# An input projection in halves of 256 columns in place of whole slabs of 512

## The chip, the core and the metric

The program runs on one NeuronCore of a Trainium2 chip, in one launch. What counts is its device time in microseconds: the median of the runs before is 2477.26 us (2477.15 and 2477.36). TensorE multiplies a stationary block (the weights, loaded by an instruction of their own) by moving columns and adds into PSUM banks of 512 float32 columns. VectorE (DVE), ScalarE (ACT) and GpSimd (POOL) do the rest of the arithmetic, and SyncE (SP) orders most of the transfers.

## The reference, cut to what matters

One layer of a decoder. The 2048 prompt tokens and 8 sample tokens are normalised, modulated and projected; the projection's columns are q, k, v, an output gate, two gate rows, u and vs. A chunked mLSTM and a gated chunk-MLP mix them, then come an output projection and a SwiGLU:

```python
h = rmsnorm(x, g_norm1) * (1 + sc1) + sh1
proj = h @ w_in
q, k, vm, o, ig, fg, u, vs = split_cols(proj, IN_SIZES)
...
x = x + gt1 * (mix @ w_out)
h2 = rmsnorm(x, g_norm2) * (1 + sc2) + sh2
a, bb = jnp.split(h2 @ w_gate_up, 2, axis=-1)
x = x + gt2 * ((jax.nn.silu(a) * bb) @ w_down)
```

Everything is float32. D_MODEL is 1024, and `w_in` without its gate columns has 3072 columns.

## The kernel before, in words

The prompt is worked through in four blocks of 512 tokens (`BLK`). Block 0 and block 3 are written out, blocks 1 and 2 are a loop over the same code. The normalised input of a block lies transposed in SBUF, as `hT`, eight tiles (`KT`) of 128 features by 512 tokens. Each float32 factor is kept as a sum of two parts of type float32r, `hi` and `lo`, and a product is made of three matmuls: lo x hi, hi x lo and hi x hi.

A **slab** is 128 columns of a weight matrix with all 1024 rows, 512 KB. SP loads it into one of two slots of `raw` (line 438); ACT rounds it into `w_hi` (line 848); DVE subtracts and gives `w_lo` (line 1337). TensorE waits for that (`slab_ready`), and for the bank to be free (`evac`), and multiplies the slab with the block's 512 tokens into one of two PSUM banks, `G[0]` or `G[1]`. For each of the eight feature tiles these are the three matmuls of `product` (lines 1862 to 1864), 24 in all with 512 moving columns each; every matmul has its own load of 128 x 128 weights. The last one signals `slab_used`, on which ACT's evacuation of the bank and the next use of the slot wait.

The input projection has 24 such slabs per block, and in block 0 the first of them is part of `first_products`, which goes its own way. The order of a block is written out in two lists, `PRE` and `MIX`: the numbers 0 to 23 are slabs (`mix_slab`), and between them stand the steps of the token mixing, among them `chunk_a` (transposes of k at line 2004, scores at 2030), `chunk_b` (lines 2039 to 2046), `spatial` (line 2061) and `finish_heads` (line 2071):

```python
PRE = [0, 1, 2, 3, "R1", 4, "V0", "R2", 5, "V1", "R3", 6, "V2", 7, "R4", "V3", 8, 9, "COL", 10, "WD", 11]
MIX = ["A0", 12, "B0", 13, "A1", 14, "B1", 15, "A2", "GV", 16, "B2", 17, "VST", 18, "A3", 19, "SO", "B3",
       20, "CMS", "CU0", 21, "CU1", "ML", 22, "CU2", 23, "CU3"]
```

So slabs fill TensorE while the other engines do the steps between. The two up projections use the same `product`, 44 slabs per block; output and down projections have a form of their own (lines 1915 to 1917) with the tokens as the stationary part. Small float32 matmuls outside these products appear in the trace as pairs of instructions, transposes as single ones. In block 3 the sample tokens' work is spread between the slabs.

Of the kernel before, what the change touches and what calls it, by code (L numbers as in the profile page):

```python
# [31 lines left out]
KT = D // P  # L32
SEQ = 2048
BLK = 512
# [73 lines left out]
def hybrid_step(nc, x_prompt, x_sample, c_prompt, c_sample, state_C, state_n, state_m, w_ada, b_ada,  # L108
# [4 lines left out]
    with ctx:  # L113
# [7 lines left out]
        def new(name, shape, dt):  # L121
            n = 4 if dt != BF16 else 2
            for s in shape[1:]:
                n *= s
            at = top[0]
            align = 128 if n >= P else 32
            at = top[0] = (at + align - 1) // align * align
            top[0] += (n + 31) // 32 * 32
            return place(name, shape, dt, at), at


        hT_hi, HT = new("hT_hi", [P, KT, BLK], F32R)
        hT_lo, HL = new("hT_lo", [P, KT, BLK], F32R)
# [8 lines left out]
        w_hi, WH = new("w_hi", [P, 2, KT, P], F32R)  # L142
        w_lo, WL = new("w_lo", [P, 2, KT, P], F32R)
# [48 lines left out]
        half, _ = new("half", [P, 32], F32)  # L192
# [89 lines left out]
        G = bank[0:2]  # L282
# [26 lines left out]
        def signal(name, per, before=0):  # L309
            return Signal(sem(name), per, before)  # L310
# [5 lines left out]
        slab_used = signal("slab_used", NSLAB, 1)  # L316
# [1408 lines left out]
        def _(pe):  # L1725
            mm = pe.matmul
# [3 lines left out]
            for k in range(KT):  # L1730
                ins = pe.transpose(T[0][:, k * R:(k + 1) * R], xs[:, k * P:(k + 1) * P], ident[0:R, 0:R])
# [124 lines left out]
            def product(out, slot, rhs_hi, rhs_lo, tiles, start=True, stop=True, before_tile=None):  # L1856

                for n, (k, r) in enumerate(tiles):
                    if before_tile is not None:
                        before_tile(k)  # L1860
                    last = n == len(tiles) - 1
                    mm(out, w_lo[:, slot, k, :], rhs_hi[:, r, :], start=start and n == 0, stop=False)  # L1862
                    mm(out, w_hi[:, slot, k, :], rhs_lo[:, r, :], start=False, stop=False)  # L1863
                    ins = mm(out, w_hi[:, slot, k, :], rhs_hi[:, r, :], start=False, stop=stop and last)  # L1864
                return ins

            every = [(k, k) for k in range(KT)]

            def raw_ready(blk, s, j=0):
                pe.wait_ge(raw_in[s % 2].sem, raw_in[s % 2].at(blk, 16 * (s // 2 + 1)) + j)  # L1870

# [57 lines left out]
            def slab_ready(blk, s, j=0):  # L1929
                pe.wait_ge(lo_done.sem, lo_done.at(blk, s + 1) + j)  # L1930
# [143 lines left out]
            def mix_slab(blk, s):  # L2074
                slab_ready(blk, s)
                if s == 0:
                    pe.wait_ge(out_read.sem, out_read.at(blk, 0))
                pe.wait_ge(evac.sem, evac.at(blk, max(s - 1, 0)))
                product(G[s % 2][:, :], s % 2, hT_hi, hT_lo, every).then_inc(slab_used.sem, 1)

            pe.sem_inc(out_read.sem, 1)
            pe.sem_inc(evac.sem, 1)
# [5 lines left out]
            def pe_block(blk, last, first=False):  # L2088
# [4 lines left out]
                for step in PRE + MIX:  # L2093
                    if isinstance(step, int):
                        if not (first and step == 0):
                            mix_slab(blk, step)
                        if first:
                            modulation(step)
                        for piece in SAMPLES.get(step, ()) if last else ():
                            for_samples(piece)  # L2100
                    elif step in ("COL", "WD", "VST", "CMS", "ML"):
                        handlers[step](blk)
                    elif step[0] == "V":
                        v_tokens(blk, int(step[1]))
                    elif step[0] == "A":
                        chunk_a(blk, int(step[1]))
                    elif step[0] == "B":
                        chunk_b(blk, int(step[1]))

                pe.wait_ge(evac.sem, evac.at(blk, N_WIN - 1))  # L2110
                for n in range(N_OUT):
                    j, q = divmod(n, OUT_Q)
                    if last:
                        if n == 0:
                            pe.wait_ge(cms_read.sem, cms_read.at(blk, H))
                            pe.wait_ge(sem("s_ready"), 1)
                        if n % 2 == 0:
                            for r in (q, q + 1):
                                raw_ready(blk, S_OUT + n + r - q)
                                sample_pairs(N2, r % 2, s_mixp, 2 * r, j, r == 0, r == OUT_Q - 1)  # L2120
                    slab_ready(blk, S_OUT + n)
                    for i in range(TT):
                        ready = None
                        if n == 0 and i == TT - 1:
                            pe.wait_ge(evac.sem, evac.at(blk, N_WIN))
                        if n < OUT_Q and i == 0:
                            def ready(k):
                                done = mix_ready if k < H else cu_ready
                                pe.wait_ge(done.sem, done.at(blk, k % H + 1))
                        if n == 0 and i == 1:  # L2130
                            pe.wait_ge(mix_ready.sem, mix_ready.at(blk, 2))
                        if n == OUT_Q:
                            pe.wait_ge(out_read.sem, out_read.at(blk, i + 1))
                        ins = tile_product(OUT_BANK[i][:, :], n % 2, mix_hi, mix_lo, 2 * q, i, q == 0,
                                           q == OUT_Q - 1, before_k=ready)
                        if q == OUT_Q - 1 and i < TT - 1:
                            ins.then_inc(tile_ps.sem, 1)
                    ins.then_inc(slab_used.sem, 1)
# [4 lines left out]
                def up_four(half_i, begin):  # L2143
                    for pair in range(2):
                        slabs, n = half_i * 4, half_i * 2
                        for u in range(2):
                            c = 2 * pair + u
                            sample_at = -1 if not last or u == 1 else 1 if begin and c == 0 else 0

                            def samples():  # L2150
                                for r in (c, c + 1):
                                    raw_ready(blk, S_UP + r, half_i * 32)
                                    sample_columns(SP_[:, r * P:(r + 1) * P], r % 2, s_hp)

                            if sample_at == 0:
                                samples()
                            slab_ready(blk, S_UP + c, slabs)
                            if u == 0:
                                pe.wait_ge(evac.sem, evac.at(blk, N_WIN + pair) + n)
                                pe.wait_ge(silu_done.sem, silu_done.at(blk, pair) + n)  # L2160
                                def ready(k):
                                    if last and begin and pair == 0 and k == KT - 2:
                                        sample_sum(EP_[:, KT * NB:])
                                    pe.wait_ge(h_ready.sem, h_ready.at(blk, k + 1))
                                product(G[0][:, :], 0, hT_hi, hT_lo, every, before_tile=ready)\
                                    .then_inc(slab_used.sem, 1)
                            else:
                                pe.wait_ge(gated.sem, gated.at(blk, pair) + n)
                                product(G[1][:, :], 1, hT_hi, hT_lo, every).then_inc(slab_used.sem, 1)
                            if sample_at == 1:  # L2170
                                pe.wait_ge(sem("s_ready"), 2)
                                samples()
# [17 lines left out]
                for n in range(N_DOWN):  # L2190
                    j, q = divmod(n, DOWN_Q)
                    def samples():
                        for r in (n, n + 1):
                            raw_ready(blk, S_DOWN + r)
                            jr, qr = divmod(r, DOWN_Q)
                            sample_pairs(SP_, r % 2, s_actp, 2 * qr, jr, qr == 0, qr == DOWN_Q - 1)
# [33 lines left out]
            for k in range(KT):  # L2230
                ins = pe.transpose(NT_BANK[k // 4][0:NB, (k % 4) * P:(k % 4 + 1) * P], s_h32[:, k, :],
                                   ident[:, :])
# [30 lines left out]
```

## Time and profile before

| | us |
|---|---|
| runs, median of 2 | 2477.26 |
| runs, lowest and highest | 2477.15, 2477.36 |
| profiled execution, span | 2477.8 |
| TensorE busy with matmuls | 2427.0 |
| TensorE busy with weight loads | 1979.9 |
| DVE busy | 1203.8 |
| ACT busy | 846.1 |
| POOL busy | 176.9 |

The profiled execution has no other time of its own than its span, from its first to its last instruction. The page gives busy times, the chain of work that ended last, and groups of instructions by line; the trace behind it answers by stretches (windows), by waits, and instruction by instruction (timeline). PE is TensorE's matmuls and PEld its weight loads, which overlap with matmuls. A matmul lasts from its start to the end of its results; neighbours overlap, so the distance of two starts, and not the duration, tells how many of them fit in a microsecond.

### The profile page before, as it was taken

The page shows a single profiled execution, that of the slowest core. Times are in us where ns is not written, and L with a number is a line of the kernel's source. Part 1 is how long each engine was busy: PE and PEld are TensorE (multiplying, and loading weights), DVE is VectorE, ACT ScalarE, POOL GpSimd, SP SyncE. Part 2 cuts the span into 40 slices and gives each one's busy share as a digit, 9 for nine tenths or more (in the row PEclk, how much of TensorE's full clock was granted, in tenths as well). Part 3 has the DMA queues.
Part 4 walks back from the last instruction along what each step waited for, and adds up shares of the span by engine and source line. Part 5 has one row for each costly group of instructions (what it writes and reads, how often), then busy time and mean ns, then how long its engine had stood idle before and what let it go on. Part 6 is the DMA issues. An engine that isn't in the chain of part 4 may idle for free.

```text
span 2477.8 us, 32788 instructions
## 1 busy us (share of the span) xinstructions
PE 2427.0 (98%) x12296; PEld 1979.9 (80%) x12296; DVE 1203.8 (49%) x1773; ACT 846.1 (34%) x1152; POOL 176.9 (7%) x143
## 2 busy tenths in 40 slices
PE   5999999999999999999999999999999999999998
PEld 4688877888888878888888878888888878888776
DVE  4648544434346554444354754443449754333323
ACT  2333422233244243334143343333236323333212
POOL 0022000000003000000002200000002400000001
PEclk8999999999999999999999999999999999999999
DMA  7822365332352333332342233333255322222222
GB/s 280 287 80 90 111 196 164 118 95 96 91 147 66 101 111 99 96 93 94 103 140 78 90 111 98 97 93 102 94 185 160 92 77 69 85 85 85 89 90 86
DMA packets 361045, 280.14 MB, mean 113 GB/s; under 512 B 11289, under 2 KB 302653, under 8 KB 360920
## 3 DMA queue, kind: packets, MB, share of 16 engines
q1 hardware_dynamic: 333012, 228.91, 30.5%
q10 hardware_dynamic: 23956, 34.81, 4.1%
q0 software_dynamic: 3968, 14.95, 1.6%
q8 instruction: 71, 1.16, 0.2%
q14 instruction: 38, 0.30, 0.0%
HBM read 267.68 MB, written 10.96 MB: 112 GB/s over the span
## 4 chain that ended last, share of the span: by engine, by line
PE 89%; DVE 5%; issue 2%; DMA 2%; ACT 1%; POOL 0%; DVEq 0%; SPq 0%; ACTq 0%; POOLq 0%
PE banks L1862 18%; PE banks L1863 18%; PE banks L1864 18%; PE banks L1915 9%; PE banks L1916 8%; PE banks L1917 8%; PE banks L1742 1%; DVE w_lo L1337 1%; DMA stage<-in_w_ada_dram 1%; PE banks L1876 1%; PE banks L2004 1%; PE banks L2061 1%; PE banks L1886 1%; PE banks L1938 1%; PE banks L2030 1%
## 5 line engine op out<-in xcount | busy, mean ns | idle before, releaser
L1862 PE MATMUL banks<-hT_hi,w_lo 128*128 128x512 f32 x2176 | 859.9, 395 | 3.1 <-DVE hT_lo L1343 1.6
L1864 PE MATMUL banks<-hT_hi,w_hi 128*128 128x512 f32 x2176 | 848.6, 390 | 0.0
L1863 PE MATMUL banks<-hT_lo,w_hi 128*128 128x512 f32 x2176 | 848.5, 390 | 0.0
L1337 DVE TENSOR_TENSOR w_lo<-raw,w_hi 128x1024 fp32r<-128x1024 f32 x392 | 493.3, 1258 | 579.5 <-ACT w_hi L848 567.7
L848 ACT ACTIVATE w_hi<-raw 128x1024 fp32r<-128x1024 f32 x392 | 412.7, 1053 | 465.7 <-PE banks L1917 437.4
L1862 PEld LDWEIGHTS banks<-hT_hi,w_lo 128*128 128x128 f32 x2176 | 409.3, 188 | 100.6 <-issue 9.3
L1864 PEld LDWEIGHTS banks<-hT_hi,w_hi 128*128 128x128 f32 x2176 | 409.0, 188 | 86.2
L1863 PEld LDWEIGHTS banks<-hT_lo,w_hi 128*128 128x128 f32 x2176 | 409.4, 188 | 81.3
L1915 PE MATMUL banks<-w_lo,act_hi 128*128 128x512 f32 x704 | 276.2, 392 | 0.0
L1916 PE MATMUL banks<-w_hi,act_lo 128*128 128x512 f32 x704 | 274.2, 390 | 0.0
L1917 PE MATMUL banks<-w_hi,act_hi 128*128 128x512 f32 x704 | 274.1, 389 | 0.0
L1675 DVE TENSOR_TENSOR work<-work,banks 128x512 f32<-128x512 f32 x88 | 60.5, 688 | 271.9 <-ACT work L971 271.9
L977 ACT ACTIVATE act_hi<-work 128x512 f32 (+1 forms) x88 | 55.6, 632 | 371.8 <-DVE work L1679 371.8
L1915 PEld LDWEIGHTS banks<-w_lo,act_hi 128*128 128x128 f32 x704 | 132.1, 188 | 32.0 <-issue 4.5
L1917 PEld LDWEIGHTS banks<-w_hi,act_hi 128*128 128x128 f32 x704 | 132.1, 188 | 27.8
L1916 PEld LDWEIGHTS banks<-w_hi,act_lo 128*128 128x128 f32 x704 | 132.2, 188 | 26.7
L1679 DVE TENSOR_TENSOR work<-work,banks 128x512 f32<-128x512 f32 x88 | 60.6, 689 | 190.1 <-PE banks L1864 190.1
L587 POOL TENSOR_TENSOR rrt<-msq,half 128x1 f32<-128x1 f32 (+1 forms) x27 | 18.2, 676 | 1424.2 <-DVE msq L1098 1168.2
L971 ACT ACTIVATE work<-banks 128x512 f32<-128x512 f32 x88 | 52.6, 598 | 187.3 <-PE banks L1864 186.9
L1915 PE MATMUL banks<-w_lo,mix_hi 128*128 128x512 f32 x256 | 100.4, 392 | 1.8 <-DVE w_lo L1337 1.1
L1916 PE MATMUL banks<-w_hi,mix_lo 128*128 128x512 f32 x256 | 99.8, 390 | 0.0
L1917 PE MATMUL banks<-w_hi,mix_hi 128*128 128x512 f32 x256 | 99.6, 389 | 0.0
(335 smaller groups left out, 1828.9 us busy)
## 6 DMA issues: line engine op xcount, KB each, us to landing
raw<-in_w_gate_up_dram SPq DMA_DIRECT2D x176, 512.0 KB, 3.6
raw<-in_w_in_dram SPq DMA_DIRECT2D x96, 512.0 KB, 3.7
raw<-in_w_down_dram SPq DMA_DIRECT2D x88, 512.0 KB, 3.6
ada_stage<-in_w_ada_dram ACTq DMA_DIRECT2D x8, 2048.0 KB
raw<-in_w_out_dram SPq DMA_DIRECT2D x32, 512.0 KB, 3.6
in_stage<-in_w_in_dram ACTq DMA_DIRECT2D x6, 2048.0 KB
stage<-in_w_ada_dram SPq DMA_DIRECT2D x4, 2048.0 KB
x_sb<-in_x_prompt_dram POOLq DMA_DIRECT2D x4, 2048.0 KB, 8.8
```

The lines of the kernel that those rows point to most:

```text
L848: act.activation(w_hi[:, s % 2], raw[:, s % 2], ACT.Copy).then_inc(hi_done.sem, 1)
L971: act.activation(work[:, 2], G[0][:, :], ACT.Sigmoid).then_inc(evac.sem, 1)
L977: act.activation(act_hi[:, bass.ds(pair_i * 2 + u, 1), :], work[:, 3:4, :], ACT.Copy)\
L1337: ve.tensor_tensor(w_lo[:, s % 2], raw[:, s % 2], w_hi[:, s % 2].bitcast(F32), ALU.subtract).then_inc(lo_done.sem, 1)
L1675: ve.tensor_tensor(work[:, 2], work[:, 2], G[0][:, :], ALU.mult).then_inc(silu_done.sem, 1)
L1679: ve.tensor_tensor(work[:, 3], work[:, 2], G[1][:, :], ALU.mult).then_inc(gated.sem, 1)
L1862: mm(out, w_lo[:, slot, k, :], rhs_hi[:, r, :], start=start and n == 0, stop=False)
L1863: mm(out, w_hi[:, slot, k, :], rhs_lo[:, r, :], start=False, stop=False)
L1864: ins = mm(out, w_hi[:, slot, k, :], rhs_hi[:, r, :], start=False, stop=stop and last)
L1915: mm(out, x_hi[:, k0 + k, t], lo[:, k, :], start=start and k == 0, stop=False)
L1916: mm(out, x_lo[:, k0 + k, t], hi[:, k, :], start=False, stop=False)
L1917: ins = mm(out, x_hi[:, k0 + k, t], hi[:, k, :], start=False, stop=stop and k == 1)
```

## The change

A new function, `half_product`, does what `product` does for a slice `t` of the block's tokens. `mix_slab` calls it twice: with tokens 0 to 255 over all eight feature tiles, then with tokens 256 to 511. Both write into their own half of the same bank, and the signal `slab_used` comes from the last matmul of the second half. A slab is then 48 matmuls of 256 moving columns, each with its own load. Each block of weights is loaded twice per slab. The first slab of block 0, the gate rows, and the output, up and down projections stay as they are.

```diff
+            def half_product(out, slot, t):
+
+                for k in range(KT):
+                    mm(out[:, t], w_lo[:, slot, k, :], hT_hi[:, k, t], start=k == 0, stop=False)
+                    mm(out[:, t], w_hi[:, slot, k, :], hT_lo[:, k, t], start=False, stop=False)
+                    ins = mm(out[:, t], w_hi[:, slot, k, :], hT_hi[:, k, t], start=False, stop=k == KT - 1)
+                return ins
+
...
                 pe.wait_ge(evac.sem, evac.at(blk, max(s - 1, 0)))
-                product(G[s % 2][:, :], s % 2, hT_hi, hT_lo, every).then_inc(slab_used.sem, 1)
+                for half in range(2):
+                    ins = half_product(G[s % 2], s % 2, slice(half * BLK // 2, (half + 1) * BLK // 2))
+                ins.then_inc(slab_used.sem, 1)
```

On TensorE, between step B0 and the next step, slab 13 of block 0 stands so before (the first row belongs to B0; w_lo and w_hi are the weights, hT the moving tokens):

```order
L2046 MATMUL banks<-vg,k_tm 128x129 x3
L1862 MATMUL banks<-hT_hi,w_lo 128x512 [waits evac,lo_done]
L1863 MATMUL banks<-hT_lo,w_hi 128x512
L1864 MATMUL banks<-hT_hi,w_hi 128x512
L1862 MATMUL banks<-hT_hi,w_lo 128x512
```

and so in the changed kernel, in which the lines behind the new function are eight higher:

```order
L2054 MATMUL banks<-vg,k_tm 128x129 x3
L1872 MATMUL banks<-hT_hi,w_lo 128x256 [waits evac,lo_done]
L1873 MATMUL banks<-hT_lo,w_hi 128x256
L1874 MATMUL banks<-hT_hi,w_hi 128x256
L1872 MATMUL banks<-hT_hi,w_lo 128x256
```

The three rows come 8 times before and 16 times now, with the waits on the first row alone; nothing stands between the halves. The order on DVE, ACT and SP is the same in both kernels.

Where the first slab of block 0 ends and the second begins, the changed kernel has, on TensorE (the rows with 512 columns are the end of `first_products`):

```order
L1863 MATMUL banks<-hT_lo,w_hi 128x512
L1864 MATMUL banks<-hT_hi,w_hi 128x512
L1759 MATMUL banks<-ident,w_raw 128x128 [waits h32,ws_masked]
L1759 MATMUL banks<-ident,w_raw 128x128 x3
L1872 MATMUL banks<-hT_hi,w_lo 128x256 [waits evac,lo_done]
```

There only the last row is new in form: it was L1862 with 128x512.

## Rows read from the trace of the kernel before

**Rows 1.** The page's first part: busy us (share), instructions of each engine.

```profile
PE 2427.0 (98%) x12296; PEld 1979.9 (80%) x12296; DVE 1203.8 (49%) x1773; ACT 846.1 (34%) x1152; POOL 176.9 (7%) x143
```

**Rows 2.** The page's chain that ended last: shares by engine, by line.

```profile
PE 89%; DVE 5%; issue 2%; DMA 2%; ACT 1%; POOL 0%; DVEq 0%; SPq 0%; ACTq 0%; POOLq 0%
PE banks L1862 18%; PE banks L1863 18%; PE banks L1864 18%; PE banks L1915 9%; PE banks L1916 8%; PE banks L1917 8%; PE banks L1742 1%; DVE w_lo L1337 1%; DMA stage<-in_w_ada_dram 1%; PE banks L1876 1%; PE banks L2004 1%; PE banks L2061 1%; PE banks L1886 1%; PE banks L1938 1%; PE banks L2030 1%
```

**Rows 3.** Windows over the input projections of block 0 and block 3.

```profile
core 0: us, PE busy (x) PEld busy (x) DVE busy (x) ACT busy (x) POOL busy (x), PEclk, DMA share, GB/s
58.86:235.73 176.87, 175.48 (x971) 136.26 (x969) 118.09 (x204) 63.38 (x92) 32.92 (x23) 0.99 0.48 151
...
1827.96:1993.25 165.29, 161.88 (x824) 135.44 (x822) 132.64 (x259) 82.90 (x142) 48.52 (x31) 0.99 0.49 150
```

**Rows 4.** TensorE's waits: waiter, whom it waited for, us, times, longest.

```profile
PE banks L2061 <- DVEq L1422: 2.6, 4, 0.7
PE banks L2046 <- POOL vg L674: 2.0, 1, 2.0
...
PE banks L1862 <- DVE w_lo L1337: 0.8, 4, 0.3
```

**Rows 5.** Timeline of TensorE in undisturbed slabs: start us, duration us, instruction.

```profile
899.65 0.39 PE L1864 MATMUL banks<-hT_hi,w_hi 128*128 128x512 f32 x1
899.88 0.39 PE L1862 MATMUL banks<-hT_hi,w_lo 128*128 128x512 f32 x1
...
944.08 0.39 PE L1862 MATMUL banks<-hT_hi,w_lo 128*128 128x512 f32 x1
```

**Rows 6.** Timeline of TensorE in slab 3 of block 0.

```profile
87.05 0.63 PE L1863 MATMUL banks<-hT_lo,w_hi 128*128 128x512 f32 x1
87.48 0.63 PE L1864 MATMUL banks<-hT_hi,w_hi 128*128 128x512 f32 x1
```

**Rows 7.** Windows around rows 5 and 6; the number behind POOL's is PEclk.

```profile
899.65:944.08 44.43, 44.43 (x198) 36.79 (x196) 18.74 (x22) 15.70 (x19) 0.00 (x0) 1.00 0.34 99
...
86.20:89.10 2.90, 2.90 (x8) 2.31 (x7) 2.55 (x5) 0.00 (x0) 0.00 (x0) 0.50 1.05 396
```

**Rows 8.** Timeline at a slab's end: its last matmul, and the next load.

```profile
92.44 0.39 PE L1864 MATMUL banks<-hT_hi,w_hi 128*128 128x512 f32 x1
...
92.76 0.12 PEld L1742 LDWEIGHTS banks<-ada_stage,hTs 128*9 128x9 f32 x8 [0.35 <-issue]
```

**Rows 9.** Timeline of small float32 matmuls with 129 and with 8 columns.

```profile
745.39 1.06 PE L2042 MATMUL banks<-CN,qT 128*128 128x129 f32 x8
746.28 1.06 PE L2046 MATMUL banks<-vg,k_tm 128*128 128x129 f32 x8
...
2079.80 0.95 PE L1904 MATMUL banks<-ssel,s_ev 128*128 128x8 f32 x8
2080.68 1.08 PE L1876 MATMUL banks<-raw,s_hp 128*32 128x128 f32 x32
```

**Rows 10.** Groups of weight loads by form: busy us, mean ns of one.

```profile
L1862 PEld LDWEIGHTS banks<-hT_hi,w_lo 128*128 128x128 f32 x2176 | 409.3, 188 | 100.6 <-issue 9.3 <-DVE hT_lo L1343 6.1 <-DVE w_lo L1337 3.2
...
L1904 PEld LDWEIGHTS banks<-ssel,s_ev 128*128 128x128 f32 x88 | 11.5, 191 | 0.8
```

**Rows 11.** Timeline: a matmul, and the load for the matmul behind it.

```profile
911.21 0.39 PE L1864 MATMUL banks<-hT_hi,w_hi 128*128 128x512 f32 x1
...
911.21 0.19 PEld L1862 LDWEIGHTS banks<-hT_hi,w_lo 128*128 128x128 f32 x1
```

**Rows 12.** Timeline of TensorE after a wait: the first and last of eleven matmuls.

```profile
1929.16 0.39 PE L1864 MATMUL banks<-hT_hi,w_hi 128*128 128x512 f32 x1
...
1931.47 0.39 PE L1862 MATMUL banks<-hT_hi,w_lo 128*128 128x512 f32 x1
```

**Rows 13.** The page's groups that split a slab on DVE and ACT.

```profile
L1337 DVE TENSOR_TENSOR w_lo<-raw,w_hi 128x1024 fp32r<-128x1024 f32 x392 | 493.3, 1258 | 579.5 <-ACT w_hi L848 567.7
L848 ACT ACTIVATE w_hi<-raw 128x1024 fp32r<-128x1024 f32 x392 | 412.7, 1053 | 465.7 <-PE banks L1917 437.4
```

## The prediction, made before the changed kernel ran

> **What bounds the kernel now.** I read the page's busy times first, then the chain of waits, then the windows of the input projections, then TensorE's waits, and last single matmuls in the timeline. TensorE is busy 98% of the span [rows 1], and the chain that ended last runs for 89% over it [rows 2]. In the stages that the change touches it is the same: TensorE works 175.48 of 176.87 us in token block 0 and 161.88 of 165.29 in block 3, while DVE, the next engine, reaches at most 132.64 [rows 3]. What it waits for there is small: 2.6 us in four places for a DVE chain (line 1422), 2.0 us once for POOL's vg, 0.8 us for four slabs whose lo part came late, 0.3 the longest [rows 4]. So a nanosecond more or less in a slab's matmuls is a nanosecond of the kernel, almost without cover.
>
> A busy PE is not yet TensorE at its peak, so the price of one matmul must be read from starts, not from the 0.39 us that it lasts. In a long stretch of undisturbed slabs the first of 197 matmuls starts at 899.65 us and the last at 944.08 [rows 5]: 44.43 / 196 = 226.7 ns per 512 columns. The granted clock is 1.00 there [rows 7], the level of 2.4 GHz, at which 512 columns need 213.3 ns. So each matmul takes **13.4 ns beyond its columns**, and the whole question is what becomes of these 13.4 ns when a matmul has 256 columns.
>
> **The change part by part.** It adds no work of arithmetic, no DMA and no wait: each slab of the steps 0 to 23 does 48 matmuls of 256 columns in place of 24 of 512, each with its own load of 128 x 128 weights. First_products keeps step 0 of block 0 as it was. That leaves 23 + 3 x 24 = 95 slabs, 95 x 24 = 2280 matmuls that become 4560.
>
> *The matmuls.* If the 13.4 ns come once per matmul, a half takes 256 / 2.4 + 13.4 = 106.7 + 13.4 = 120.0 ns, a pair 240.0, and the change costs 2280 x (240.0 - 226.7) = **+30.4 us**. If they come with the columns, a half takes 113.3 ns and the change costs nothing. Three rows bear on it. In a stretch in which the granted clock is 0.50 [rows 7], the level of 1.2 GHz, the same matmuls start 0.43 us apart [rows 6]: that is 512 / 1.2 = 427 ns with nothing on top. So the 13.4 ns are no cycles of the array, neither per matmul nor per column; something that feeds the array needs about 227 ns and shows only at the full clock. And it is not the load of the next weights that gets in the way: the last matmul before some small ones, with no load behind it for 0.35 us, still lasts 0.39 us [rows 8]. After an interruption the distance is larger before it settles: ten steps from 1929.16 to 1931.47 us, 231 ns each [rows 12]. A rate per column would hardly change so, a start-up of each matmul could; I take the fixed cost, and keep the rate as a rival.
>
> *The loads.* A load begins when the matmul before it begins [rows 11] and today has 226.7 ns; it will have 120. Nearest rows: eight matmuls of 8 columns each take 2080.68 - 2079.80 = 0.88 us, eight of 129 columns 0.89 us [rows 9], 110 to 111 ns each, each with its own 128 x 128 load. With so different columns the same distance means that the load sets it. These are plain float32, but their loads last as long, 191 ns against 188 [rows 10]. So loads follow each other every 111 ns, which fits under 120 with 9 ns to spare: nothing added. The bounds of a half are then 111 ns (below, if the 13.4 ns vanish beside the load) and 129 ns (above, 111 and then 231 - 213.3 = 17.7, if the start-up follows the load and never settles).
>
> *Issue.* TensorE gets 2280 more pairs of load and matmul. The rows with 129 columns issue a pair in 111 ns [rows 9]; at 120 this is covered, and at worst it is the same 111.
>
> *The neighbours.* The semaphores fire where they did, after the last matmul of a slab, so ACT evacuates the whole bank as before. A slab grows from 24 x 226.7 = 5.44 to 5.76 us. Splitting the next one takes 1.05 us on ACT and 1.26 on DVE [rows 13], and its raw data was ordered one slab earlier: more covered than before, cost nothing; without that cover a late slab would cost at most those 2.3 us. What a longer slab gives back is waits: in front of line 2061 one slab lies between the DVE chain's start and its use, so 4 x 0.32 = 1.3 us, the longest late lo part 0.3, and POOL's vg up to 2.0 [rows 4]. Between nothing and -3.6 us I take **-2.5**, since POOL's chain is in part tied to DVE's order in the same slabs.
>
> *Sum.* +30.4 - 2.5 = +28 us on the profiled execution's span of 2477.8, 2505.7 us. Its span lies 0.5 us over the median of the runs, 2477.26, so **2505 us**, 1.1% more. A change of 2% is 49.5 us; about that is what a measurement of this kernel can tell from no change.
>
> **The rule against it.** The row says 226.7 ns for 512 columns, 13.4 more than they need. The Trainium skill, TensorE: Matmul & The Clock Gate, section Back-to-back issue gap, gives a warm matmul N / 2.4 + 2.5 ns, 216 for 512 columns; the trace disagrees by 11 ns. By that rule a half would take 109.2 ns, an estimate, and the load would be the longer of the two. What that would do here is the second rival.
>
> **The rivals.**
> 1. *The extra is a rate.* 113.3 ns per half, 0 us for the matmuls, -1 for waits: 2476. For it speaks that a matmul with no load behind it is stretched as much as the others [rows 8]; against it the unequal 231 and 227 ns [rows 5, 12].
> 2. *The loads set the pace, a little faster.* If a half carries almost no start-up, it waits for its load: 111.5 ns, 223 a pair, 2280 x -3.7 = -8 us, 2469. For it speak the narrow matmuls, in which nothing beyond the load shows [rows 9]; against it that the start-up of float32r at full clock is seen in every settled row [rows 5].
> 3. *The start-up comes behind the load: slower.* Today the next load is long done when a matmul ends; with 111 ns of load beside 107 of columns it is the last to arrive, and if a matmul's start-up can only begin then, a half takes 111 + 13.4 = 124 ns, or 129 with the 17.7 ns of the unsettled steps [rows 12]. Place: each half of the 95 slabs. Price: with the middle, 126.5, a pair takes 253, 2280 x 26.3 = +60, less 2.5 for waits, 2535 (2525 to 2545 with the two ends). It decides from 125 ns per half: then 4560 x 4.8 = 22 us come on top of 2505 and 2% are reached. For it speaks that nothing in the rows shows a float32r matmul that waits for its load; against it that rows of 129 columns, as close to their loads, keep an even 111 [rows 9].
> 4. *Load and matmul follow each other.* 111 + 120 = 231 per half, 2280 x 235 = +537 us, 3014. Against it stand rows 9, with half that distance.
>
> That the change does not do what it says is out: the order shows 256 columns in all of these slabs.
>
> **How the numbers follow.** The fixed cost, 2505: 0.58. Rival 1, 2476: 0.20. Rival 2, 2469: 0.06. Rival 3, 2535: 0.12. Rival 4: 0.04. The likeliest gives the predicted time; its own range is 2503 to 2508 (waits between -3.6 and nothing, on 2477.3 + 30.4). The range over the cases goes from 2469 (rival 2) to 2535 (the middle of rival 3) and leaves out half of rival 3, rival 4 and what lies under rival 2. Within 2%: the fixed cost, rivals 1 and 2, and the lower end of rival 3, which crosses the border at 2527: 0.87. Slower by over 2%: the rest of rival 3 and rival 4: 0.12. Faster by over 2%: no row shows a way to -50 us; 0.01.
>
> **What would show it.** In the changed kernel's timeline the starts within an input slab should be 120 ns apart, a slab 5.76 us long, and the 512-column stages unchanged at 226.7 ns. Loads should start with the matmul before them, 188 ns long, and not end the wait of a matmul. The windows of the four projections should be longer by 7 to 8 us each, and the waits on lines 2061 and 2046 (of before) shorter. Starts 113 ns apart make rival 1 right, 111 with matmuls lengthened by their loads rival 2, 124 to 129 rival 3. The prediction is wrong in its central step if the half's extra is not 13 ns.

## The result, and the profile after

The changed kernel takes 2499.86 us (2499.14 and 2500.58) against 2477.26: ratio 1.0086, interval 1.0056 to 1.0115. That is 22.6 us more, where 28 were predicted; the profiled executions, 2477.8 and 2499.1 us, differ by 21.3. The forecast of 2505 us is 5 us high: the time lies within the range over the cases, 2469 to 2535, and 3 us under the likeliest case's own, 2503 to 2508. The mechanism behind it did not hold in the same way: the 13 ns per half are there, but they are no fixed cost of a matmul, and the weight loads have a part in them.

First the page of the changed kernel: busy times, the chain that ended last by engine and by line, and one of the new lines' groups.

```profile
PE 2452.6 (98%) x14576; PEld 2101.1 (84%) x14576; DVE 1211.8 (48%) x1773; ACT 846.3 (34%) x1152; POOL 170.5 (7%) x143
...
PE 91%; DVE 4%; issue 2%; DMA 2%; ACT 1%; POOL 0%; DVEq 0%; SPq 0%; ACTq 0%; POOLq 0%
...
L1872 PE MATMUL banks<-hT_hi,w_lo 128*128 128x256 f32 x1520 | 436.2, 287 | 1.1 <-DVE w_lo L1337 1.0
...
L1872 PEld LDWEIGHTS banks<-hT_hi,w_lo 128*128 128x128 f32 x1520 | 291.3, 192 | 2.7 <-DVE w_lo L1337 1.6
```

There are 2280 more matmuls and as many more loads than in [rows 1], and the chain runs over TensorE for 91% where it was 89% [rows 2]. A load lasts 192 ns, 188 before [rows 10].

The price is read from starts. In the timeline of TensorE (start us, duration us, instruction) the first two rows are the ends of 24 undisturbed steps in a slab of block 1, the last two those of 190 steps in an up projection:

```profile
677.02 0.28 PE L1872 MATMUL banks<-hT_hi,w_lo 128*128 128x256 f32 x1
...
679.90 0.28 PE L1872 MATMUL banks<-hT_hi,w_lo 128*128 128x256 f32 x1
...
899.80 0.39 PE L1862 MATMUL banks<-hT_hi,w_lo 128*128 128x512 f32 x1
...
942.88 0.39 PE L1863 MATMUL banks<-hT_lo,w_hi 128*128 128x512 f32 x1
```

2.88 / 24 = 120.0 ns per half, and 43.08 / 190 = 226.7 ns per 512 columns, as in [rows 5]. Of all 4560 halves, 4106 are followed by the next matmul after 120 ns. So a pair costs 240.0 - 226.7 = 13.3 ns, and 2280 pairs 30.4 us, as the prediction had it.

Timeline of the weight loads in the same slab:

```profile
676.91 0.19 PEld L1872 LDWEIGHTS banks<-hT_hi,w_lo 128*128 128x128 f32 x1
677.03 0.19 PEld L1873 LDWEIGHTS banks<-hT_lo,w_hi 128*128 128x128 f32 x1
```

The matmul of line 1872 starts at 677.02 and the load for the next one, of line 1873, at 677.03: load and matmul start together, as in [rows 11]. The next matmul starts at 677.14, before the 0.19 us of its load are over on record, so that duration can't tell whether a matmul waits for its load. In a kernel with matmuls of 128 columns (below) they start some 60 ns after their loads; here it is 117, so the halves are not held back by their own loads in that way.

TensorE's waits after (waiter, whom it waited for, us, times, longest), where they changed:

```profile
PE banks L1742 <- DMA stage<-in_w_ada_dram: 12.4, 3, 7.6
...
PE banks L2069 <- DVEq L1422: 1.2, 3, 0.4
PE banks L1872 <- DVE w_lo L1337: 1.0, 1, 1.0
PE banks L2054 <- POOL vg L674: 0.9, 1, 0.9
```

Lines 2069 and 2054 are 2061 and 2046 of before. The DVE chain's 2.6 us fell to 1.2 and POOL's 2.0 to 0.9 [rows 4]. The wait for the adaptive weights, at the very start, was 9.8 us in two places before and is 12.4 in three; a third one of 3.1 us was put down to DVE before.

Last the windows (us; then busy time and count of PE, PEld, DVE, ACT, POOL; granted clock; DMA share; GB/s): the projection of block 0, the slab of block 0 in which [rows 6] lie, and the projection of block 3.

```profile
60.31:241.05 180.74, 179.82 (x1520) 165.23 (x1519) 120.01 (x204) 63.38 (x92) 29.88 (x23) 1.00 0.47 148
87.60:90.50 2.90, 2.90 (x25) 2.90 (x26) 2.58 (x4) 0.00 (x0) 0.00 (x0) 1.00 0.96 350
1845.60:2014.95 169.35, 166.87 (x1399) 165.22 (x1397) 135.44 (x260) 83.06 (x142) 50.52 (x31) 1.00 0.48 146
```

The two projections take 180.74 and 169.35 us against 176.87 and 165.29 [rows 3], 3.9 and 4.1 more. The middle row stands for something that was not in the sum: before, the granted clock was 0.50 here (1.2 GHz) [rows 7], after it is 1.00 (2.4 GHz). In the trace of before TensorE had just done small matmuls and a wait of 0.57 us; block 3 had a second such stretch, after the wait of 2.0 us for POOL:

```profile
1925.70:1929.10 3.40, 3.40 (x13) 3.03 (x13) 1.75 (x3) 0.00 (x0) 3.32 (x4) 0.50 0.55 148
```

In these two stretches 512 columns started 427 ns apart instead of 227, and in the second the small matmuls of line 2046 were slower too, some 1.6 us lost in each. The changed kernel's profiled execution has neither.

**Where the time went.** From the first gate matmul to the first one of the output projection the four blocks grew by 3.84, 6.16, 6.07 and 4.06 us, 20.1 together; the start before them grew by 1.45, the end lost 0.45, and the stages between grew by 0.13. In the start it is not the waits for the adaptive weights, 12.9 us before with the one on DVE and 12.4 after: the three groups of 16 matmuls on these weights took 10.7 us against 9.1. The change doesn't touch them, and why they took longer is not shown. Of the four blocks' 20.1 us, +30.4 are the pairs; -3.7 are TensorE's waits there, 8.4 us before and 4.7 after; -3.2 are the two stretches at the lower clock. The rest, -3.4, is seen in the steps after each interruption, which have not yet settled to one distance. In the input projections of before, 388 such steps of 512 columns took 231.5 ns on average, 1.9 us in all over 226.7; after, 325 such halves took 118.2, 0.6 us in all under 120.0. That makes -2.5; the other -0.9 lies in the first and last steps of the slabs, beside other matmuls. Two of the rows:

```profile
1845.60 0.28 PE L1872 MATMUL banks<-hT_hi,w_lo 128*128 128x256 f32 x1
...
1846.90 0.28 PE L1874 MATMUL banks<-hT_hi,w_hi 128*128 128x256 f32 x1
```

These are 11 steps, some 118 ns each, behind the gate matmuls of block 3; the unsettled steps of [rows 12] took 231. A settled pair costs 13.3 ns, an unsettled one 2 x 118.2 - 231.5 = 4.9. Block 1 has no stretch at the lower clock and is closed by itself: 576 x 13.33 = 7.68 for the pairs, -0.54 for unsettled steps, -0.82 for waits, -0.16 for first and last steps and the small matmuls, together 6.16, by which the block grew.

### The profile page after: what moved, and what is told of

Read it like the earlier page. It is cut to its first block, busy times and chain, and to the rows that moved or that the text cites. A ratio compares the mean times of both kernels' runs of the same rounds, so it can differ in the third digit from the quotient of the medians.

```text
span 2499.1 us, 37348 instructions
## 1 busy us (share of the span) xinstructions
PE 2452.6 (98%) x14576; PEld 2101.1 (84%) x14576; DVE 1211.8 (48%) x1773; ACT 846.3 (34%) x1152; POOL 170.5 (7%) x143
## 4 chain that ended last, share of the span: by engine, by line
PE 91%; DVE 4%; issue 2%; DMA 2%; ACT 1%; POOL 0%; DVEq 0%; SPq 0%; ACTq 0%; POOLq 0%
PE banks L1862 13%; PE banks L1863 13%; PE banks L1864 13%; PE banks L1923 9%; PE banks L1925 8%; PE banks L1924 8%; PE banks L1872 6%; PE banks L1874 6%; PE banks L1873 6%; PE banks L1742 1%; DMA stage<-in_w_ada_dram 1%; PE banks L1884 1%; DMA raw<-in_w_in_dram 1%; DVE w_lo L1337 1%; PE banks L2012 1%
## 5 line engine op out<-in xcount | busy, mean ns | idle before, releaser
L1862 PE MATMUL banks<-hT_hi,w_lo 128*128 128x512 f32 x1416 | 556.0, 393 | 2.9 <-DVE hT_lo L1343 1.6
L1863 PE MATMUL banks<-hT_lo,w_hi 128*128 128x512 f32 x1416 | 551.2, 389 | 0.0
L1864 PE MATMUL banks<-hT_hi,w_hi 128*128 128x512 f32 x1416 | 551.2, 389 | 0.0
L1872 PE MATMUL banks<-hT_hi,w_lo 128*128 128x256 f32 x1520 | 436.2, 287 | 1.1 <-DVE w_lo L1337 1.0
L1874 PE MATMUL banks<-hT_hi,w_hi 128*128 128x256 f32 x1520 | 429.9, 283 | 0.0
L1873 PE MATMUL banks<-hT_lo,w_hi 128*128 128x256 f32 x1520 | 429.9, 283 | 0.0
L1862 PEld LDWEIGHTS banks<-hT_hi,w_lo 128*128 128x128 f32 x1416 | 265.8, 188 | 71.1 <-issue 8.5
L1864 PEld LDWEIGHTS banks<-hT_hi,w_hi 128*128 128x128 f32 x1416 | 265.8, 188 | 55.6
L1863 PEld LDWEIGHTS banks<-hT_lo,w_hi 128*128 128x128 f32 x1416 | 265.9, 188 | 53.4
L1872 PEld LDWEIGHTS banks<-hT_hi,w_lo 128*128 128x128 f32 x1520 | 291.3, 192 | 2.7 <-DVE w_lo L1337 1.6
L1873 PEld LDWEIGHTS banks<-hT_lo,w_hi 128*128 128x128 f32 x1520 | 291.5, 192 | 0.1
L1874 PEld LDWEIGHTS banks<-hT_hi,w_hi 128*128 128x128 f32 x1520 | 291.3, 192 | 0.0
L1675 DVE TENSOR_TENSOR work<-work,banks 128x512 f32<-128x512 f32 x88 | 60.6, 688 | 271.9 <-ACT work L971 271.9
```

The costliest lines, as they stand in the source:

```text
L1675: ve.tensor_tensor(work[:, 2], work[:, 2], G[0][:, :], ALU.mult).then_inc(silu_done.sem, 1)
L1872: mm(out[:, t], w_lo[:, slot, k, :], hT_hi[:, k, t], start=k == 0, stop=False)
L1873: mm(out[:, t], w_hi[:, slot, k, :], hT_lo[:, k, t], start=False, stop=False)
L1874: ins = mm(out[:, t], w_hi[:, slot, k, :], hT_hi[:, k, t], start=False, stop=k == KT - 1)
```

## The experiments

They were to tell whether the 13.3 ns of a pair are a start-up of each matmul, a pace of the loads, or something else, and whether the order of the halves or the place in the block matters. In all of them the slabs of the input projection alone are changed, unless the text says otherwise, and in the block order of before. A settled distance is one that repeats, within 1 ns, through a run of equal matmuls; steps that hold an interruption are left out of the means.

**The change once more**, beside kernels that do a part of it. No edit: it is the changed kernel.

> The changed kernel again, beside the kernel before, for a narrower interval: 21 to 24 us slower. If the shares that I read from the two traces are right (2280 matmuls doubled at +13.3 ns a pair, +30.4 us; less about 3 to 4 us of waits, about 3 us of stretches at the half clock, about 3 us of settling after interruptions), its trace shows the same shares again, and the stretch at a granted clock of 0.50 in slab 3 of block 0 is missing again.

2498.99 us against 2479.69, ratio 1.0082 (1.0065 to 1.0099), +19.3. The blocks grew by 3.81, 6.14, 6.05 and 1.32 us: the same as above but in block 3, where TensorE's waits are 0.5 us against 2.4 in the first execution of the changed kernel and 3.4 in that of before. So the change costs 19 to 23 us, less than the 21 to 24 expected here, and block 3 carries most of the scatter. The stretch at 0.50 in block 0 is missing again. (It lies in slab 4, the first behind the step R1; [rows 6] and the expectations call it slab 3.)

**Half of the slabs in halves**, the first twelve of a block or the last twelve:

```diff
-                product(G[s % 2][:, :], s % 2, hT_hi, hT_lo, every).then_inc(slab_used.sem, 1)
+                for lo, hi in ((0, 256), (256, 512)) if s < 12 else ((0, 512),):
+                    ins = half_product(G[s % 2], s % 2, slice(lo, hi))
+                ins.then_inc(slab_used.sem, 1)
```

> Halves only in slabs 0 to 11, the ones ahead of the token mixing; slabs 12 to 23 whole, as before. Start-up theory: 47 slabs x 24 x 13.3 ns = +15.0 us. The slabs of this part are interrupted about as often as the others, so they get back 1 to 2 us of settling, and the stretch at the half clock in slab 3 of block 0 (1.5 us) if that is due to the halves. Little of the waits, which lie behind slab 19: about +12 us, 2489. If the waits are shortened by slabs anywhere ahead of them, +10.

2490.25 us, ratio 1.0043 (1.0027 to 1.0060), +10.6. The waits in front of lines 2069 and 2054, which lie among the whole slabs, are as before, 2.6 and 2.0 us.

```diff
+                for lo, hi in ((0, 256), (256, 512)) if s >= 12 else ((0, 512),):
```

> Halves only in slabs 12 to 23, between the steps of the mixing. Start-up theory: 48 slabs x 24 x 13.3 ns = +15.4 us; less the waits at lines 2061 and 1915, about 0.8 us per block, less settling of 1 to 2 us: about +10.5, 2488. Together with the run of slabs 0 to 11 it should give what all halves cost, 22 to 23; a large difference would mean that the two parts share a cause that I do not see.

2489.55 us, ratio 1.0039 (1.0025 to 1.0053), +9.9. The two parts make 20.4 together, the whole 19.3 beside them: the cost goes with the number of halved slabs, not with their place. The wait at line 2069 is 1.3 us here, as in the changed kernel, but POOL's at 2054 is 2.0, as before, although the slabs around it are halved: it shrinks only where all are. The sum was expected at 22 to 23, the cost as first measured. One more thing was open, whether the missing stretch at the lower clock is due to the halves. This kernel's first twelve slabs are whole, as before, and yet:

```profile
85.90:89.30 3.40, 3.40 (x17) 2.77 (x16) 3.00 (x7) 0.00 (x0) 0.00 (x0) 1.00 1.05 400
```

The granted clock is 1.00 there, with the same work before it. So the stretch at 0.50 that before's trace has in this place comes and goes between executions; its absence after is not shown to be the change's doing.

**The halves in turns:** for each block of weights the left half, then the right, so that the same weights are loaded twice in a row.

```diff
+                for k in range(KT):
+                    for w, x in ((w_lo, hT_hi), (w_hi, hT_lo), (w_hi, hT_hi)):
+                        for t in halves:
+                            ins = mm(G[s % 2][:, t], w[:, s % 2, k, :], x[:, k, t],
...
```

> The halves take turns: for each block of weights first the left half of the tokens, then the right, so that the same weights are loaded twice in a row. Start-up theory: the order of the halves is of no account, 120 ns each, about +20 us, the ratio of the changed kernel within 0.3%. If the chip leaves out the second load of the same weights, or reads them faster, the starts could come under 120 ns only if the load had a share in them: by the theory load pace (120 ns because of loads) two halves with one load between them would come to 2 x 109 = 218 to 227 ns, -20 to 0 us.

2498.48 us, ratio 1.0080 (1.0063 to 1.0097), as the halves one after the other. The starts are 120 ns apart, every repeated load is still carried out, and the order of the halves is of no account.

**Other widths.** Slabs in turn whole, as 320 + 192, as 384 + 128, and as four times 128 columns:

```diff
+            SPLITS = [((0, 512),), ((0, 320), (320, 512)), ((0, 384), (384, 512)),
+                      ((0, 128), (128, 256), (256, 384), (384, 512))]
...
+                for lo, hi in SPLITS[s % 4]:
+                    ins = half_product(G[s % 2], s % 2, slice(lo, hi))
```

> Slabs 0, 4, 8 ... whole; 1, 5, 9 ... in 320 + 192 columns; 2, 6, 10 ... in 384 + 128; 3, 7, 11 ... in four quarters of 128. Theory start-up (each float32r matmul takes its columns / 2.4 + 13.3 ns, or the pace of loads, 112 ns, if that is longer): starts 227 ns after a matmul of 512 columns, 173 after 384, 147 after 320, and 112 after 192 and 128. Theory load pace (a half waits 120 ns for its load, and the extra of 512 columns is a rate of 6%): 170 after 384, 142 after 320, 120 after 192 and after 128. In all about +179 us by the first, less 5 to 10 for waits and settling (2647 to 2651), about +202 by the second (2670 to 2675).

2642.44 us in one run, 5 under the first theory's range and 28 under the second's. The timeline of TensorE, the first and last of 23 steps of 320 columns, of 16 steps of 128, and of 15 steps of 384:

```profile
715.48 0.30 PE L1872 MATMUL banks<-hT_hi,w_lo 128*128 128x320 f32 x1
...
718.85 0.31 PE L1874 MATMUL banks<-hT_hi,w_hi 128*128 128x320 f32 x1
...
727.14 0.28 PE L1872 MATMUL banks<-hT_hi,w_lo 128*128 128x128 f32 x1
...
728.92 0.28 PE L1873 MATMUL banks<-hT_lo,w_hi 128*128 128x128 f32 x1
...
753.20 0.33 PE L1874 MATMUL banks<-hT_hi,w_hi 128*128 128x384 f32 x1
...
755.80 0.33 PE L1874 MATMUL banks<-hT_hi,w_hi 128*128 128x384 f32 x1
```

146.5, 111 and 173.3 ns. With 320 and 384 columns the extra is 13.3 ns again (146.7 - 133.3, 173.3 - 160), which a fixed cost foretells and a rate does not. Matmuls of 128 columns start as fast as their loads, 111.7 ns over all of them, 192 columns on average 111.8; so loads can follow each other closer than 120 ns. So far the fixed cost had won. But 128 and 192 columns hide behind the loads, and there the theory had not been tried.

**Narrow loads.** To uncover the short matmuls, the next three kernels load only a part of the 128 weight columns in some slabs. Those slabs leave out the outputs of the other weight columns; the number of moving columns is as it would be. So a narrow load goes together with fewer output rows, and these runs can't tell the two apart. First 64 of 128, in the odd slabs:

```diff
+            def half_product(out, slot, t, m):
...
+                    mm(out[0:m, t], w_lo[:, slot, k, 0:m], hT_hi[:, k, t], start=k == 0, stop=False)
...
+                    ins = half_product(G[s % 2], s % 2, slice(lo, hi), P // 2 if s % 2 else P)
```

> Odd slabs load 64 of their 128 weight columns only, so the other half of their outputs is left out; slabs 1, 5, 9 ... with 512 moving columns, 3, 7, 11 ... in quarters of 128. Even slabs load all 128: 0, 4, 8 ... whole, 2, 6, 10 ... in halves. If the 13.3 ns come with the moving columns' own start, they stay with a narrow load: 227 ns per 512 columns, and a quarter, freed from the 112 ns of its load, comes to 128 / 2.4 + 13.3 = 67 ns. If they come from the load (its reads, or the change of the weights), they shrink with it: 220 ns or less per 512, and a quarter at half a load's pace, 56 to 60 ns. By a pace of issue of a pair of load and matmul, a quarter would stay near 110.

2489.97 us. A quarter with a load of 64 columns (the tile reads 128*64), 50 steps, and 512 columns with such a load, 12 steps:

```profile
736.47 0.22 PE L1872 MATMUL banks<-hT_hi,w_lo 128*64 128x128 f32 x1
...
739.47 0.22 PE L1874 MATMUL banks<-hT_hi,w_hi 128*64 128x128 f32 x1
...
678.06 0.39 PE L1872 MATMUL banks<-hT_hi,w_lo 128*64 128x512 f32 x1
...
680.82 0.39 PE L1872 MATMUL banks<-hT_hi,w_lo 128*64 128x512 f32 x1
```

3.00 / 50 = 60.0 ns. The fixed cost says 53.3 + 13.4 = 66.7, a rate 56.7; both miss, and the 60.0 lie at the upper end of what was expected if the extra comes from the load. But by that 512 columns should have taken 220 or less, and they take 2.76 / 12 = 230.0 ns, with 224, 230 and 236 in turns, and never settle at 226.7. This is the run in which the fixed cost fell.

**Narrower loads**, 32 columns for most, 64 for the halves:

```diff
+            SPLITS = [((0, 512),), ((0, 256), (256, 512)), ((0, 192), (192, 384), (384, 512)),
+                      ((0, 128), (128, 256), (256, 384), (384, 512))]
+            WIDE = [32, 64, 32, 32]
```

> Still fewer of the 128 weight columns are loaded, so most outputs of the input projection are left out: 32 in slabs 0, 4, 8 ... (512 moving columns), 64 in 1, 5, 9 ... (two halves of 256), 32 in 2, 6, 10 ... (192 + 192 + 128) and 3, 7, 11 ... (four quarters of 128). With 64 loaded columns a quarter came to 60 ns and not to 67, so the extra of 13.3 ns fails for 128 columns, or a quarter is held by something else. If the extra grows with the columns up to 256 (6.7 ns at 128) and then stays: 60 ns per 128, 90 per 192, 120 per 256, 227 to 231 per 512. If it is 13.3 ns for all and the 60 ns were an error of reading: 67, 93, 120, 227. If it depends on the load: with 64 columns loaded a half comes under 120 (107 to 115), with 32 a quarter under 60. If a pair of load and matmul needs 60 ns to be issued, a quarter stays at 60 and the 192 show which of the first two holds.

2486.04 us. The timeline, 29 steps of halves with a load of 64, and 10 steps of 512 columns with a load of 32:

```profile
698.60 0.28 PE L1874 MATMUL banks<-hT_hi,w_hi 128*64 128x256 f32 x1
...
701.89 0.28 PE L1873 MATMUL banks<-hT_lo,w_hi 128*64 128x256 f32 x1
...
741.06 0.39 PE L1873 MATMUL banks<-hT_lo,w_hi 128*32 128x512 f32 x1
...
743.37 0.40 PE L1874 MATMUL banks<-hT_hi,w_hi 128*32 128x512 f32 x1
```

The same 256 columns that settle at 120.0 ns behind loads of 128 settle at 3.29 / 29 = 113.4 behind loads of 64. A pair of them takes 226.7 ns, less than the 230.0 of 512 columns behind loads of 64: there the split costs nothing. And 512 columns behind loads of 32 take 231 ns and stay there (mean 231.4 over all). 192 columns take 88.4 ns on average, 128 take 60.0. So the settled distance belongs neither to the matmul nor to its columns alone.

**A line?** The unsettled means of these runs lie near 3 + 0.447 ns per moving column. This kernel was made to try that at other widths, where the line and 13.4 ns per matmul part:

```diff
+            SPLITS = [((0, 256), (256, 512)), ((0, 256), (256, 512)), ((0, 320), (320, 512)), ((0, 448), (448, 512))]
+            WIDE = [32, 96, 32, 32]
```

> Again fewer weight columns are loaded and most outputs of the input projection are left out: 32 of 128 in slabs 0, 4, 8 ... (two halves of 256), 96 in 1, 5, 9 ... (two halves), 32 in 2, 6, 10 ... (320 + 192) and in 3, 7, 11 ... (448 + 64). So far the starts that have not settled to one distance lie on a line, 60.3 ns for 128 columns, 89.5 for 192, 118 for 256, 231.5 for 512, about 3 + 0.447 ns per column, whatever is loaded beside them; the settled ones lie on multiples of 6.67 ns (113.3, 120.0, 146.7, 173.3, 226.7). Theory line and steps: 146 per 320 columns, 203.5 per 448, 89 per 192, about 32 per 64 unless issue needs more; a half 117 to 118 where it does not settle, 113.3 or 120.0 where it does, with 96 loaded columns as with 32. Theory fixed extra of 13.3 ns from 256 columns on, less with narrow loads: 120 with 96 loaded columns, 113 or less with 32; 147 per 320 and 200 per 448.

2487.49 us. The timeline, 42 steps of 256 columns behind loads of 96, then behind loads of 32 21 steps of 320, 10 of 448 and 11 of 64:

```profile
676.84 0.28 PE L1874 MATMUL banks<-hT_hi,w_hi 128*96 128x256 f32 x1
...
681.71 0.27 PE L1874 MATMUL banks<-hT_hi,w_hi 128*96 128x256 f32 x1
...
681.97 0.30 PE L1873 MATMUL banks<-hT_lo,w_hi 128*32 128x320 f32 x1
...
684.98 0.31 PE L1873 MATMUL banks<-hT_lo,w_hi 128*32 128x320 f32 x1
...
690.03 0.36 PE L1873 MATMUL banks<-hT_lo,w_hi 128*32 128x448 f32 x1
...
692.05 0.36 PE L1874 MATMUL banks<-hT_hi,w_hi 128*32 128x448 f32 x1
...
739.37 0.19 PE L1872 MATMUL banks<-hT_hi,w_lo 128*32 128x64 f32 x1
...
739.72 0.19 PE L1874 MATMUL banks<-hT_hi,w_hi 128*32 128x64 f32 x1
```

116.0, 143.3, 202 and 31.8 ns; over all their steps 116.1, 144.4, 202.4 and 32.2. The line gives 117.4, 146.0, 203.3 and 31.6, the fixed cost 120.0, 146.7, 200.0 and 40.0. So the line holds within 1.6 ns, nearer than the fixed cost at all four; but 320 columns lie at 143.3 to 143.5 ns in 17 of 24 slabs and at 146.4 to 146.7 in the others, and 256 columns behind loads of 32 settle at 113.3 in 12 of 23 slabs and run at 117.8 in the rest. One and the same matmul and load came out both ways within one kernel. All float32r distances side by side, in ns:

| moving columns | columns / 2.4 | line | free running (weight columns loaded) | settled (weight columns loaded) |
|---|---|---|---|---|
| 64 | 26.7 | 31.6 | 32.2 (32) | |
| 128 | 53.3 | 60.2 | 60.0 (32), 60.0 (64) | 60.0 (32 and 64, in some slabs) |
| 192 | 80.0 | 88.8 | 88.4 (32) | |
| 256 | 106.7 | 117.4 | 117.8 (32), 116.0 (96), 118.2 (128, after interruptions) | 113.3 (64; 32 in half of the slabs), 116.7 (96, in two slabs), 120.0 (128) |
| 320 | 133.3 | 146.0 | 141 to 147 in some slabs (32) | 143.3 and 146.7 in other slabs (32), 146.7 (128) |
| 384 | 160.0 | 174.6 | 177 (128, after interruptions) | 173.3 (128) |
| 448 | 186.7 | 203.3 | 202.4 (32) | |
| 512 | 213.3 | 231.9 | 230.1 (64), 231.4 (32), 231.5 (128, after interruptions) | 226.7 (128) |

The settled values 60.0, 113.3, 120.0, 146.7, 173.3 and 226.7 are multiples of 6.67 ns, as was expected; 116.7 and 143.3 were not, and lie halfway between two such multiples. All are multiples of 3.33.

**Another type of number.** All hi and lo parts are bfloat16 instead of float32r, which is coarser; odd slabs in halves, even ones whole.

```diff
-        w_hi, WH = new("w_hi", [P, 2, KT, P], F32R)
+        _, WH = new("w_hi_room", [P, 2, KT, P], F32)
+        w_hi = place("w_hi", [P, 2, KT, P], BF16, WH)
...
+                for lo, hi in ((0, 256), (256, 512)) if s % 2 else ((0, 512),):
```

> All float32r tiles of the products (weights, hT, mix, act and the gate weights, each as a hi and a lo part) are bfloat16 here, so the products are coarser; odd slabs of the input projection come in halves of 256 columns, even ones whole. If the 13.3 ns are float32r's (its moving columns have twice the bytes), a matmul of 512 columns takes about 216 ns and a half about 109, and the kernel about 9472 x 10.9 = 103 us less than the one before, plus 48 x 24 x 2.5 ns = 3 us for the halves: about 2375. If they belong to every matmul with a load of 128 x 128 weights before it, 227 and 120 ns as in float32r, about 2487.

2380.28 us. Timeline, 40 steps of a half:

```profile
670.53 0.27 PE L1879 MATMUL banks<-hT_hi,w_lo 128*128 128x256 bf16 x1
...
674.90 0.27 PE L1880 MATMUL banks<-hT_lo,w_hi 128*128 128x256 bf16 x1
```

109.2 ns, and 215.8 for 512 columns: 2.5 ns beyond the columns, in both, with no settling. A pair costs 2.6 ns here, a fifth of what it costs in float32r. So most of the 13 ns belongs to the type; whether to that of the moving columns or to that of the weights is not told apart, since both changed.

**bfloat16 parts with whole slabs**, the kernel before in everything else:

> The same in bfloat16 parts with all slabs whole, as in the kernel before. float32r's start-up: 216 ns per 512 columns, 2477 - 103 = 2374, a few us less where DVE's and ACT's smaller outputs shorten waits, so 2365 to 2376. A start-up of every matmul: 2470 to 2477.

2379.95 us, ratio 0.9599 (0.9583 to 0.9615): 99 us less than before, and faster than both kernels. The first and the last of 69 matmuls, and TensorE's waits:

```profile
654.73 0.38 PE L1879 MATMUL banks<-hT_hi,w_lo 128*128 128x512 bf16 x1
...
669.40 0.38 PE L1881 MATMUL banks<-hT_hi,w_hi 128*128 128x512 bf16 x1
```

```profile
PE banks L1749 <- DMA stage<-in_w_ada_dram: 13.1, 3, 7.7
PE banks L1953 <- DVE dg L1123: 6.1, 8, 1.0
...
PE banks L2076 <- DVEq L1429: 5.1, 4, 1.3
PE banks L1879 <- DVE w_lo L1344: 3.6, 3, 2.9
PE banks L1869 <- DVE hT_lo L1350: 3.3, 8, 1.6
```

14.67 / 68 = 215.7 ns against 226.7. It stayed 4 us short of what was expected. Faster slabs uncover waits: line 2076 (2061 of before) waits 5.1 us for its DVE chain where it waited 2.6, and line 1879 waits 3.6 for lo parts where line 1862 waited 0.8 [rows 4]. Beside the 2380.28 of the kernel before this one, halves make no difference that can be seen in bfloat16.

## Why the prediction was right, and where it was not

**What bounds the kernel: right.** The change made TensorE's matmuls longer, and the time followed: in block 1 the pairs' 7.68 us, less what its waits and unsettled steps gave back, are the growth.

**The step that failed** is in the paragraph on the matmuls: "A rate per column would hardly change so, a start-up of each matmul could; I take the fixed cost". The number it gave, 120.0 ns per half, was measured to the digit, and with loads of 128 so were 146.7 and 173.3; but 13.4 ns is no constant of a matmul. Behind narrow loads 256 columns take 113.3, 116 or 118, 128 take 60.0 instead of 66.7, and 512 take 230 to 231 instead of 226.7. That the half came out at the forecast digit was in this sense luck. What the runs show in its place is a free pace of about 3 ns and 0.447 ns per column, and settled distances near it. By that, the 13.3 ns of a pair can be put down to three places. Two free halves against one free whole are 2 x 117.8 - 231.4 = 4.2 ns (both behind loads of 32). The whole had settled at 226.7, 4.7 below its free pace, and that is lost. And each half settles at 120.0, 2.2 above its free pace, 4.4 for both. So about two thirds of the price hang on where the two sizes happened to settle. The paragraph on the loads failed with it: "nothing added". The loads fit under 120 ns, as it says, but behind loads of 64 the same halves settle at 113.3, 6.7 ns less, and a pair costs no more than a whole. The hints were in the trace of before. The unsettled 231 ns [rows 12] was read as a start-up that had not yet settled, when it is the free pace. And the 427 ns at the lower clock [rows 6], with nothing on top, leave no room for a cost that always comes on top of the columns, while a pace of 231 ns disappears under them.

**Rival 1, a rate, was half true.** Most of the extra of a free matmul of 512 columns is a rate, 0.447 - 0.417 = 0.03 ns per column; but taken from 226.7 it gave 113.3 and nothing to pay, and behind loads of 128 the halves settle elsewhere. The matmul without a load behind it [rows 8] could not speak for it: the same 0.39 us stand beside starts 227 and 231 ns apart [rows 5, 12]. Rivals 2, 3 and 4 fell: no run of halves settles at 111, 124 to 129 or 231 ns.

**The rule that was weighed.** The bfloat16 rows show 215.8 and 109.2 ns for 512 and 256 columns. The Trainium skill, TensorE: Matmul & The Clock Gate, section Back-to-back issue gap, gives N / 2.4 + 2.5 ns for a warm matmul, by which 512 and 256 columns would take 215.8 and 109.2, an estimate. There the trace agrees. For float32r, 226.7 and 120.0, it disagrees, and the measurement decides.

**Issue and neighbours: right, and the loads' own pace.** Loads of 128 follow each other every 111.7 ns on average, read before from 110 to 111 [rows 9], and fit under 120; that they add nothing is what failed. Issue was covered with far more room than shown before: pairs of load and matmul follow each other every 32 ns in the last of the narrow kernels. The 1.05 and 1.26 us of splitting a slab [rows 13] stayed hidden but for one late lo part of 1.0 us.

**Waits: right places, size too small.** -2.5 was taken between nothing and -3.6; in the four blocks they gave back 3.7, of which 1.7 is 0.57 us in each of three blocks that TensorE had lost before the first slab of the output projection (line 1915), a place that was not on the list. Its rows in the waits of before have none to answer them after:

```profile
PE banks L1915 <- DVE w_lo L1337: 1.1, 2, 0.6
...
PE banks L1915 <- issue: 0.6, 1, 0.6
```

**What the sum left out.** The two stretches at the lower clock, -3.2, and the unsettled, first and last steps, -3.4: the first stretch was seen [rows 6, 7] and used for its rate, but not asked whether it comes each time. For these reasons and the waits the projections grew by 4 to 6 us and not by 7 to 8. Against them the start grew by 1.45 us. 30.4 - 3.7 - 3.2 - 3.4 + 1.45 - 0.45 + 0.13 gives the spans' 21.3 within 0.1, where +28 was said.

**Still open.** What decides whether and where a run of float32r matmuls settles. The width of the load, or of the output that goes with it, takes part: 256 moving columns always settle at 120.0 with 128 weight columns and at 113.3 with 64, in two of 24 slabs with 96 (116.7), and in half of the slabs with 32 (113.3). So the width alone doesn't decide. Why that is so was not tried.

## What to carry to other kernels

Before calling the time beyond a matmul's columns a fixed cost or a rate, measure it at a second and third width, and behind a load that is out of its way; one distance in one settled run is consistent with both. Keep float32r matmuls at 512 columns where loads are 128 wide, and read from the starts whether they have settled; where the accuracy of bfloat16 parts suffices, they save 4% of this kernel. Ask of each stretch at a lower clock in a profile whether another execution has it too, before any part of a difference is put down to it.

## What the runs showed of the hardware

- The settled distances of float32r matmuls in these runs lie on multiples of 3.33 ns, most of them of 6.67, and a settled run may be faster (226.7 against 231.4 for 512 columns) or slower (120.0 against 117.8 for 256) than the free pace.
- The width of the weight load (and of the output with it) changes the distance of the matmuls, although loads alone can follow each other every 111.7 ns: 120.0 ns for 256 columns behind loads of 128, 113.3 behind loads of 64.
- Loading the same weights again costs as much as loading others: in the kernel with turns each of the 48 loads of a slab is carried out, and lasts 192 ns as in the changed kernel.
- bfloat16 takes 2.5 ns beyond its columns with either width, float32r 13.3 where it has settled behind loads of 128.
